# A hybrid convolution and mixture-of-experts layer: the first block of three product stages taken chunk by chunk, both token halves together

## The chip, the cores and the metric

The kernel runs on one core of one Trainium2 chip. The metric is the device time of one execution in microseconds. The kernel before has a median of 1347.25 us over three runs (1346.16 to 1347.42). All times in this text come from those runs or from one profiled execution of the kernel before.

## The reference

One layer of a decoder trunk is computed for 520 tokens of width 1024 (512 of a prompt, 8 single sample tokens), in float32:

```python
h = rmsnorm(x, g_pre1) * (1 + sc1) + sh1
z = h @ w_in                          # 1024 -> 7 * 1024: a_in a_b a_c b_val b_gate g_a g_b
v = causal_dwconv3(a_c * a_in)
y_a = (a_b * v) @ w_out_a
cv = causal_dwconv31(b_val * sigmoid(b_gate)) + b_cconv
y_b = silu(layernorm(cv)) @ w_out_b + b_out_b
m = sigmoid(g_a) * y_a + sigmoid(g_b) * y_b
t = m @ w_o
x = x + gt1 * rmsnorm(t, g_post1)
h = rmsnorm(x, g_pre2) * (1 + sc2) + sh2
x = x + gt2 * rmsnorm(moe(h), g_post2)   # 64 experts, top 8, one shared expert
```

`sc1`, `sh1`, `gt1` and their second set come from `silu(c) @ w_ada + b_ada`, per sequence.

## The kernel before

Channels lie on the 128 partitions, in C = 8 chunks of 128; the 520 tokens lie along the free axis and are taken in two halves of 260 (`half`), one PSUM bank each.

Every large matrix of the first part (`w_in`, `w_out_a`, `w_out_b`, `w_o`) is used in blocks: a block is 1024 input channels by 128 output channels. There are 80 of them, numbered n: 0 to 55 for `w_in` (four passes of a loop of 14, called f = 0 to 13), 56 to 63 for `w_out_a`, 64 to 71 for `w_out_b`, 72 to 79 for `w_o`. A block's weights come by DMA into `raw`; ScalarE copies them rounded into the high part (`split_hi`, L648), GpSimd subtracts to get the low part (`split_lo`, L460). Two such pairs fit in `wsplit`.

The activations are split in the same way, chunk by chunk, into a high and a low tensor of the product's type:

- for `w_in`: VectorE applies scale and shift (L974), ScalarE rounds (`h_hi`, L655, counted by `h_act`), VectorE subtracts (`h_lo`, L979, counted by `h_lo_dve`);
- for `w_out_a`: GpSimd multiplies `va` (L466), ScalarE rounds (`va_hi`, L669, `va_hi_act`), GpSimd subtracts (`va_lo`, L471, `va_lo_pool`);
- for `w_o`: VectorE makes the rounded sum (`m_hi`, L1089), the full sum (L1090) and the difference (`m_lo`, L1092, `m_lo_dve`).

A block is computed by `split_product` as three products per chunk and half (high x high, low x high, high x low; L1396, L1397, L1398), which makes 3 x 8 x 2 = 48 matmuls of 260 columns. It does the whole first half (24 matmuls into one bank), and then the whole second half (24 into the next bank). The blocks alternate between banks 0/1 and 2/3. For blocks f = 0 and 56 the first half waits before each chunk until that chunk's low part is there; block 72 waits for all eight low parts before its first matmul.

After block 0 TensorE computes a part of the conditioning (`ada_chunk`, L1349), which waits for four copies by ScalarE (`stB_act`, L660), and after block 56 the channel means of the convolution (`stat`, L1337), which wait for a small VectorE product (`p2_dve`, L1046).

Each engine has its own instruction stream in program order, and the streams meet only in semaphores. Nothing reorders the matmuls: the order is the order of the code.

## Time and profile before

| | |
|---|---|
| median of 3 runs | 1347.25 us |
| the profiled execution | 1346.86 us, of which the span of the profile is 1345.1 us |
| TensorE busy | 1258.6 us (94%), 9215 matmuls |
| VectorE, ScalarE, GpSimd busy | 500.5 (37%), 351.3 (26%), 368.3 us (27%) |
| the 80 blocks | from 58.1 to about 585 us |
| the expert part | from about 656 to 1273 us |

The profile shows times of one execution. Matmuls are pipelined: a record lasts about 0.28 us at the full clock, while the next one starts 0.12 us later, so spacing is read from the starts. "Granted clock" (PEclk) is the share of full speed that TensorE was given. "Idle before" is the time for which an engine had nothing to do ahead of an instruction, with what ended it.

### The profile page before, as it was taken

Reading aid. Unit: us, or ns where it says so; the run is one execution under the profiler, and the core shown is the slowest. Engines: PE = TensorE matmul, PEld = TensorE weight load, DVE = VectorE, ACT = ScalarE, POOL = GpSimd, SP = SyncE. Lnnn points to the kernel's source line nnn. Section 1 sums busy time; section 2 is a strip of 40 time slices with the busy share of each in tenths; the row PEclk is TensorE's granted clock in tenths of the full one; section 3 lists DMA queues with packets and bytes.
Section 4 is the critical chain, followed back from the end, with each engine's and each line's share of the span. In section 5 each row is a group of like instructions: output and inputs, shape, how many; then the busy total and the mean of one; then the engine's idle time right before and its main releaser. Section 6 shows DMA issues by size and latency. Waiting matters only on the chain.

```text
span 1345.1 us, 26176 instructions
## 1 busy us (share of the span) xinstructions
PE 1258.6 (94%) x9215; PEld 936.2 (70%) x9216; DVE 500.5 (37%) x857; ACT 351.3 (26%) x644; POOL 368.3 (27%) x370
## 2 busy tenths in 40 slices
PE   6799999999998998978898999998999999999985
PEld 4599999999998898967654555554555555555532
DVE  0556677566865557048412111100011100110067
ACT  4332332323232611335211122112122112211221
POOL 1144444444564333301311122112122112211200
PEclk8699999999999998989999999999999999999998
DMA  9944262443411232309599899999999999995186
GB/s 308 262 148 151 79 217 82 152 140 94 140 47 48 73 98 78 95 21 387 216 417 366 319 392 411 391 418 418 417 418 399 402 346 419 418 409 196 49 303 268
DMA packets 155591, 336.72 MB, mean 250 GB/s; under 512 B 12445, under 2 KB 96925, under 8 KB 137078
## 3 DMA queue, kind: packets, MB, share of 16 engines
q1 hardware_dynamic: 137888, 295.00, 58.6%
q0 software_dynamic: 14256, 34.10, 6.7%
q10 hardware_dynamic: 3406, 7.05, 1.6%
q8 instruction: 28, 0.46, 0.1%
q14 instruction: 13, 0.11, 0.0%
HBM read 321.65 MB, written 33.26 MB: 264 GB/s over the span
## 4 chain that ended last, share of the span: by engine, by line
PE 79%; DMA 6%; issue 5%; DVE 5%; ACT 2%; POOL 1%; SPq 1%; ACTq 0%; DVEq 0%; POOLq 0%
PE ps L1579 25%; PE ps L1591 13%; PE ps L1396 10%; PE ps L1397 10%; PE ps L1398 10%; PE ps L1572 4%; PE ps L1337 2%; PE ps L1525 2%; DMA w<-in_w_dram 2%; DMA ring<-in_w_ada_dram 2%; PE ps L1349 1%; PE ps L1585 1%; SPq L281 1%; DVE ring L1300 1%; POOL wsplit L460 1%
## 5 line engine op out<-in xcount | busy, mean ns | idle before, releaser
L1579 PE MATMUL ps<-w,xe 128*64 x3136 | 353.5, 384 | 21.9 <-issue 21.9
L1579 PEld LDWEIGHTS ps<-w,xe 128*64 128x64 f32 x3136 | 229.4, 139 | 161.3 <-issue 59.9
L1396 PE MATMUL ps<-h_s_hi,wsplit 128*128 128x260 f32 x1024 | 292.1, 285 | 2.8 <-DVE h_lo_m_hi L979 2.7
L1398 PE MATMUL ps<-h_s_hi,wsplit 128*128 128x260 f32 x1024 | 289.7, 283 | 0.0
L460 POOL TENSOR_TENSOR wsplit<-ring,wsplit 128x1024 fp32r<-128x1024 f32 x80 | 192.3, 2404 | 321.8 <-ACT wsplit L648 321.8
L1397 PE MATMUL ps<-h_lo_m_hi,wsplit 128*128 128x260 f32 x896 | 253.9, 283 | 0.0
L1266 DVE TENSOR_TENSOR rs<-sg,ps 128x128 f32<-128x128 f32 x98 | 23.8, 284 | 495.5 <-PE ps L1579 495.5
L1396 PEld LDWEIGHTS ps<-h_s_hi,wsplit 128*128 128x128 f32 x1024 | 193.6, 189 | 11.2 <-issue 6.7
L1398 PEld LDWEIGHTS ps<-h_s_hi,wsplit 128*128 128x128 f32 x1024 | 194.0, 189 | 0.0
L1591 PE MATMUL ps<-w,eactT 128*64 (+1 forms) x784 | 179.0, 598 | 0.0
L1397 PEld LDWEIGHTS ps<-h_lo_m_hi,wsplit 128*128 128x128 f32 x896 | 169.8, 190 | 0.0
L648 ACT ACTIVATE wsplit<-ring 128x1024 fp32r<-128x1024 f32 x80 | 84.8, 1060 | 322.2 <-PE ps L1398 314.9
L1014 DVE SCALAR_TENSOR_TENSOR ps<-conv,vecs,ps 128x512 f32<-128x512 f32 x224 | 154.6, 744 | 0.0
L532 POOL COPY gidx<-idxT 128x1 int32 (+1 forms) x50 | 9.2, 185 | 408.7 <-PE ps L1572 407.3
L1591 PEld LDWEIGHTS ps<-w,eactT 128*64 128x64 f32 x784 | 52.1, 136 | 89.8 <-issue 84.0
L883 ACT ACTIVATE act<-ps 128x1024 f32<-128x1024 f32 x50 | 51.2, 1024 | 162.9 <-PE ps L1591 160.4
L898 ACT ACTIVATE eactT<-ps 128x128 f32<-128x128 f32 x98 | 23.3, 278 | 188.5 <-PE ps L1585 188.5
L1572 PE MATMUL ps<-ident,scr 128*128 128x128 f32 x400 | 65.8, 287 | 0.0
L1572 PEld LDWEIGHTS ps<-ident,scr 128*128 128x128 f32 x400 | 52.3, 193 | 18.9 <-issue 17.7
L535 POOL DMA_INDIRECT scr<-h_rows,gidx x50 | 53.0, 1061 | 40.5 <-POOL gidx L532 40.5
L545 POOL DMA_INDIRECT y_rows<-act,sidx x49 | 49.9, 1019 | 40.3 <-POOL sidx L542 39.5
L895 ACT ACTIVATE sg<-ps 128x256 f32<-128x256 f32 x49 | 18.9, 385 | 148.3 <-PE ps L1579 148.3
(286 smaller groups left out, 1402.6 us busy)
## 6 DMA issues: line engine op xcount, KB each, us to landing
w<-in_w_dram SPq DMA_DIRECT2D x192, 1024.0 KB, 17.2
ring<-in_w_in_dram SPq DMA_DIRECT2D x56, 512.0 KB, 3.9
ring<-in_w_ada_dram SPq DMA_DIRECT2D x12, 2048.0 KB, 9.7
ring<-y_rows SPq DMA_DIRECT2D x8, 1024.0 KB, 9.3
act<-y_rows SPq DMA_DIRECT2D x8, 1024.0 KB, 13.9
ring<-in_w_out_a_dram SPq DMA_DIRECT2D x8, 512.0 KB, 3.6
ring<-in_w_out_b_dram SPq DMA_DIRECT2D x8, 512.0 KB, 3.7
ring<-in_w_o_dram SPq DMA_DIRECT2D x8, 512.0 KB, 3.6
```

The lines of the kernel that those rows point to most:

```text
L460: pool.tensor_tensor(wsplit[:, b, 1], raw[raw_slot], wsplit[:, b, 0], ALU.subtract).then_inc(S["w_lo"], 1)
L535: pool.indirect_dma_start(out=xg, out_offset=None, in_=h2_rows, in_offset=bass.IndirectOffsetOnAxis(ap=gidx[:, u:u + 1], axis=0), bounds_c ...
L545: pool.indirect_dma_start(out=y_rows, out_offset=bass.IndirectOffsetOnAxis(ap=sidx[:, u:u + 1], axis=0), in_=yb[:, u, :], in_offset=None, ...
L648: act.activation(wsplit[:, b, 0], raw[raw_slot], ACT.Copy).then_inc(S["w_hi"], 1)
L883: act.activation(yb[:, 1 - u, :], ps[:, 4:6, :].rearrange("p b n -> p (b n)"), ACT.Copy).then_inc(S["ex_yd"], 1)
L1014: chain(stt(out=acc[k % 2] if k != KC - 2 else cvj, in0=glu[:, k:k + NP], scalar=vecs[:, ds(j + (V_WC + 8 * k), 1)], in1=acc[k % 2], op0=A ...
L1396: mm(ps[:, bank + h, 0:HT], wsplit[:, b, 0, k, :], hi[:, k, p:q], start=(k == 0), stop=False)
L1397: mm(ps[:, bank + h, 0:HT], wsplit[:, b, 0, k, :], lo[:, k, p:q], start=False, stop=False)
L1398: ins = mm(ps[:, bank + h, 0:HT], wsplit[:, b, 1, k, :], hi[:, k, p:q], start=False, stop=(k == C - 1))
L1572: ins = tr(ps[:, h, (c % 4) * P:(c % 4 + 1) * P], v[:, c, :], ident[:, :])
L1579: ins = mm(ps[a * STRIP:(a + 1) * STRIP, bank, 0:FE], xe[:, k, a * STRIP:(a + 1) * STRIP], w[a][:, k, :], start=(k == 0), stop=(k == C - 1))
L1591: ins = mm(ps[a * STRIP:(a + 1) * STRIP, 4 + h, :], eactT[:, k, a * STRIP:(a + 1) * STRIP], w[a][:, k, h * 512:(h + 1) * 512], start=(k == ...
```

## The change

A new helper, `first_product`, replaces `split_product` for block f = 0 of each of the four passes of the loop, for block 56 and for block 72. For each chunk it issues first the four matmuls that need only the high part of the activations (two weight parts times two halves), after a wait for the chunk's high part, and then the two matmuls (two halves) that need the low part, after a wait for the low part. With `apart=3` (block 56) the low parts of the last three chunks come after all high ones. Block 72 no longer waits for all of `m_lo`, and its wait for the last merged chunk (`m_done` 17) moves to the block after it. One increment is added to a VectorE instruction (`m_hi_dve`), and one wait (`h_s_dve`) ahead of the loop. The number of matmuls, their sizes and operands are the same.

```diff
--- before.py
+++ after.py
@@ -249,7 +249,7 @@
                  "mean_pe cen_dve lrt_act ln_dve s_act x1_dve x1n_dve h2_act h2_s_dve logits_pe "
                  "lt_act score0_dve score_s_act mask_dve rank_pe idx_dve table_dve late_chain t_dve "
                  "g_done m_done m_chain t_cp stat_mm sqd idx_ab idx_mm hx_T hx_done "
-                 "x1t_T x1t_done x1t_dve h2_dve oneE_dve token_act turn_pool sh_mm sh_ev sh_act "
+                 "m_hi_dve x1t_T x1t_done x1t_dve h2_dve oneE_dve token_act turn_pool sh_mm sh_ev sh_act "
                  "exT xe_act xe_dve ex1 ex3 ex_sil ex_mul exA ea_act "
                  "ex_y ex_yd gcopy scopy passed yb_free es_dve es_pe y_there "
                  "diag_act yacc fin_sq fin_rt fin_out").split()
@@ -1086,7 +1086,7 @@
                             scalar=vecs[:, ds(j + V_OB, 1)], in1=gb[:, ds(j, 1), a:b].rearrange("p c t -> p (c t)"),
                             op0=ALU.add, op1=ALU.mult).then_inc(S["m_chain"], 1)
                     dve.wait_ge(S["m_chain"], j * 2 + 6)
-                    tt(hj, mj, gj, ALU.add)
+                    tt(hj, mj, gj, ALU.add).then_inc(S["m_hi_dve"], 1)
                     tt(mj, mj, gj, ALU.add).then_inc(S["m_done"], 1)
                     dve.wait_ge(S["m_done"], j + 10)
                     tt(m_lo[:, ds(j, 1), :].rearrange("p a t -> p (a t)"), mj, hj, ALU.subtract).then_inc(S["m_lo_dve"], 1)
@@ -1386,16 +1386,38 @@
                         ins = mm(ps[:, bank + h, 0:HT], w[:, k, :], src[:, k, a:b], start=(k == 0), stop=(k == C - 1))
                 return ins
 
-            def split_product(n, b, bank, hi, lo, as_they_come=None):
+            def split_product(n, b, bank, hi, lo):
 
                 pe.wait_ge(S["w_lo"], n + NU + 1)
                 for h, (p, q) in enumerate(half):
                     for k in range(C):
-                        if as_they_come and h == 0:
-                            pe.wait_ge(S[as_they_come], k + 1)
                         mm(ps[:, bank + h, 0:HT], wsplit[:, b, 0, k, :], hi[:, k, p:q], start=(k == 0), stop=False)
                         mm(ps[:, bank + h, 0:HT], wsplit[:, b, 0, k, :], lo[:, k, p:q], start=False, stop=False)
                         ins = mm(ps[:, bank + h, 0:HT], wsplit[:, b, 1, k, :], hi[:, k, p:q], start=False, stop=(k == C - 1))
+                ins.then_inc(items_used, 1)
+
+            def first_product(n, b, bank, hi, lo, hi_done, lo_done, apart=0):
+
+                pe.wait_ge(S["w_lo"], n + NU + 1)
+
+                def high(k):
+                    pe.wait_ge(S[hi_done], k + 1)
+                    for a in range(2):
+                        for h, (p, q) in enumerate(half):
+                            mm(ps[:, bank + h, 0:HT], wsplit[:, b, a, k, :], hi[:, k, p:q], start=(k == 0 and a == 0), stop=False)
+
+                def low(k):
+                    pe.wait_ge(S[lo_done], k + 1)
+                    for h, (p, q) in enumerate(half):
+                        ins = mm(ps[:, bank + h, 0:HT], wsplit[:, b, 0, k, :], lo[:, k, p:q], start=False, stop=(k == C - 1))
+                    return ins
+
+                for k in range(C):
+                    high(k)
+                    if k < C - apart:
+                        ins = low(k)
+                for k in range(C - apart, C):
+                    ins = low(k)
                 ins.then_inc(items_used, 1)
 
 
@@ -1413,6 +1435,7 @@
                     ins = mm(ps[:, 5, at:at + NSEQ], arow[:, n * P:(n + 1) * P], fold[:, :], start=True, stop=True)
                 ins.then_inc(S["ada_T"], 1)
 
+            pe.wait_ge(S["h_s_dve"], 1)
             with pe.Fori(0, C // 2) as it:
                 for jj in range(2):
                     j = it * 2 + jj
@@ -1434,11 +1457,17 @@
                             ada_chunk(it * 32 + 32, it * 2 + 5)
                         elif jj == 1 and i == 1:
                             ada_turn(1, it * 2 + 6)
-                        split_product(it * 14 + f, f % 2, 2 * (f % 2), h_hi, h_lo, "h_lo_dve" if f == 0 else None)
+                        if f == 0:
+                            first_product(it * 14, 0, 0, h_hi, h_lo, "h_act", "h_lo_dve")
+                        else:
+                            split_product(it * 14 + f, f % 2, 2 * (f % 2), h_hi, h_lo)
 
             for j in range(C):
                 pe.wait_ge(S["g_done"] if j < 2 else S["m_done"], 17 + j if j < 2 else j)
-                split_product(56 + j, j % 2, 2 * (j % 2), va_hi, va_lo, "va_lo_pool" if j == 0 else None)
+                if j == 0:
+                    first_product(56, 0, 0, va_hi, va_lo, "va_hi_act", "va_lo_pool", apart=3)
+                else:
+                    split_product(56 + j, j % 2, 2 * (j % 2), va_hi, va_lo)
                 if j == 0:
                     pe.wait_ge(S["p2_dve"], 1)
                     for c in range(C):
@@ -1464,14 +1493,17 @@
                     pe.wait_ge(S["m_chain"], it * 8 + (2 * jj + 2))
                     split_product(it * 4 + (64 + jj), jj % 2, 2 * (jj % 2), s_hi, cv_lo)
 
-            pe.wait_ge(S["m_lo_dve"], C)
-            pe.wait_ge(S["m_done"], 17)
+            pe.wait_ge(S["m_done"], 16)
             pe.wait_ge(S["tailrows_act"], 2)
             for j in range(C + 1):
                 if j < C:
                     if j >= 2:
                         pe.wait_ge(S["t_cp"], j)
-                    split_product(72 + j, j % 2, 2 * (j % 2), m_hi, m_lo)
+                    if j == 0:
+                        first_product(72, 0, 0, m_hi, m_lo, "m_hi_dve", "m_lo_dve")
+                    else:
+                        pe.wait_ge(S["m_done"], 17)
+                        split_product(72 + j, j % 2, 2 * (j % 2), m_hi, m_lo)
                 if j > 0:
                     pe.wait_ge(S["sqd"], 8 + j)
                     stat(6, scr[:, (j - 1) % 4, :], j - 1).then_inc(S["stat_mm"], 1)
```

What TensorE issues at the start of block 0, before: three matmuls for a chunk, all of the first half, `h_s_hi` being `h_hi` and `h_lo_m_hi` being `h_lo`.

```order
L1396 MATMUL ps<-h_s_hi,wsplit 128x260 [waits h_lo_dve,w_lo]
L1397 MATMUL ps<-h_lo_m_hi,wsplit 128x260
L1398 MATMUL ps<-h_s_hi,wsplit 128x260
L1396 MATMUL ps<-h_s_hi,wsplit 128x260 [waits h_lo_dve]
L1397 MATMUL ps<-h_lo_m_hi,wsplit 128x260
L1398 MATMUL ps<-h_s_hi,wsplit 128x260
L1396 MATMUL ps<-h_s_hi,wsplit 128x260 [waits h_lo_dve]
L1397 MATMUL ps<-h_lo_m_hi,wsplit 128x260
L1398 MATMUL ps<-h_s_hi,wsplit 128x260
```

And after the change: four matmuls on the high part, then two on the low part, both halves.

```order
L1407 MATMUL ps<-h_s_hi,wsplit 128x260 [waits h_act,w_lo]
L1407 MATMUL ps<-h_s_hi,wsplit 128x260 x3
L1412 MATMUL ps<-h_lo_m_hi,wsplit 128x260 [waits h_lo_dve]
L1412 MATMUL ps<-h_lo_m_hi,wsplit 128x260
L1407 MATMUL ps<-h_s_hi,wsplit 128x260 [waits h_act]
L1407 MATMUL ps<-h_s_hi,wsplit 128x260 x3
L1412 MATMUL ps<-h_lo_m_hi,wsplit 128x260 [waits h_lo_dve]
L1412 MATMUL ps<-h_lo_m_hi,wsplit 128x260
```

The second half's matmuls have moved from behind chunk 7 of the first half into each chunk, and the first four of a chunk no longer wait for the low part.

Block 56 on TensorE, before: its last waiting chunk (7), behind which the second half begins in the fourth row.

```order
L1396 MATMUL ps<-va_hi,wsplit 128x260 [waits va_lo_pool]
L1397 MATMUL ps<-va_lo,wsplit 128x260
L1398 MATMUL ps<-va_hi,wsplit 128x260
L1396 MATMUL ps<-va_hi,wsplit 128x260
L1397 MATMUL ps<-va_lo,wsplit 128x260
```

And after the change, from the high products of chunk 6 on, to the channel means behind the block.

```order
L1407 MATMUL ps<-va_hi,wsplit 128x260 [waits va_hi_act]
L1407 MATMUL ps<-va_hi,wsplit 128x260 x3
L1407 MATMUL ps<-va_hi,wsplit 128x260 [waits va_hi_act]
L1407 MATMUL ps<-va_hi,wsplit 128x260 x3
L1412 MATMUL ps<-va_lo,wsplit 128x260 [waits va_lo_pool]
L1412 MATMUL ps<-va_lo,wsplit 128x260
L1412 MATMUL ps<-va_lo,wsplit 128x260 [waits va_lo_pool]
L1412 MATMUL ps<-va_lo,wsplit 128x260
L1412 MATMUL ps<-va_lo,wsplit 128x260 [waits va_lo_pool]
L1412 MATMUL ps<-va_lo,wsplit 128x260
L1337 MATMUL ps<-act,avg 128x260 [waits p2_dve]
```

Behind the wait for the last low part stand two matmuls now, where before 27 stood.

The beginning of block 72 on TensorE, before; here `h_lo_m_hi` is `m_hi`, and the one wait stands for all eight chunks.

```order
L1396 MATMUL ps<-h_lo_m_hi,wsplit 128x260 [waits tailrows_act,w_lo,m_done,m_lo_dve]
L1397 MATMUL ps<-m_lo,wsplit 128x260
L1398 MATMUL ps<-h_lo_m_hi,wsplit 128x260
L1396 MATMUL ps<-h_lo_m_hi,wsplit 128x260
L1397 MATMUL ps<-m_lo,wsplit 128x260
```

And after the change.

```order
L1407 MATMUL ps<-h_lo_m_hi,wsplit 128x260 [waits w_lo,m_hi_dve,tailrows_act,m_done]
L1407 MATMUL ps<-h_lo_m_hi,wsplit 128x260 x3
L1412 MATMUL ps<-m_lo,wsplit 128x260 [waits m_lo_dve]
L1412 MATMUL ps<-m_lo,wsplit 128x260
L1407 MATMUL ps<-h_lo_m_hi,wsplit 128x260 [waits m_hi_dve]
L1407 MATMUL ps<-h_lo_m_hi,wsplit 128x260 x3
L1412 MATMUL ps<-m_lo,wsplit 128x260 [waits m_lo_dve]
L1412 MATMUL ps<-m_lo,wsplit 128x260
```

The wait for the eighth low part has moved from ahead of the 48 matmuls to ahead of the last two. The streams of VectorE, ScalarE and GpSimd hold the same instructions in the same order before and after.

## Rows read from the trace of the kernel before

**Rows 1.** Waits, TensorE: in total, times, longest (us).

```profile
PE ps L1396 <- DVE m_lo L1092: 5.6, 1, 5.6
PE ps L1396 <- POOL va_lo L471: 4.6, 2, 4.0
PE ps L1396 <- DVE h_lo_m_hi L979: 2.7, 3, 1.9
```

**Rows 2.** Timeline, block 0: start, us, engine, line, [idle before <-releaser].

```profile
52.82 3.43 PE L1379 MATMUL ps<-ident,act 120*128 120x120 f32 x16 [0.82 <-issue]
54.89 1.66 ACT L655 ACTIVATE h_s_hi<-act 128x512 fp32r<-128x512 f32 x3
55.60 2.37 DVE L979 TENSOR_TENSOR h_lo_m_hi<-act,h_s_hi 128x520 fp32r<-128x520 f32 x1 [0.86 <-ACT h_s_hi L655]
62.62 1.91 DVE L979 TENSOR_TENSOR h_lo_m_hi<-act,h_s_hi 128x520 fp32r<-128x520 f32 x3
63.73 1.48 ACT L660 ACTIVATE act<-ps 128x480 f32<-128x480 f32 x3
64.18 0.42 PE L1396 MATMUL ps<-h_s_hi,wsplit 128*128 128x260 f32 x1
65.48 0.42 PE L1396 MATMUL ps<-h_s_hi,wsplit 128*128 128x260 f32 x1
68.99 1.92 PE L1349 MATMUL ps<-ring,scT 128*32 128x512 f32 x16
```

**Rows 3.** Stretches: PE, PEld, DVE, ACT, POOL busy, PEclk, DMA, GB/s.

```profile
58.12:68.99 10.87, 9.90 (x48) 8.45 (x48) 6.41 (x12) 5.01 (x9) 0.00 (x0) 0.69 1.02 282
407.55:419.81 12.26, 7.69 (x50) 7.27 (x49) 7.31 (x12) 2.78 (x5) 6.10 (x4) 0.86 0.29 87
531.09:538.40 7.31, 7.31 (x49) 7.31 (x50) 0.45 (x3) 0.00 (x0) 0.00 (x0) 0.78 0.15 44
538.40:544.14 5.74, 5.74 (x50) 5.74 (x49) 0.00 (x0) 2.25 (x4) 2.40 (x1) 1.00 0.11 33
59.50:60.00 0.50, 0.22 (x2) 0.01 (x1) 0.50 (x1) 0.47 (x1) 0.00 (x0) 0.83 1.17 286
414.50:415.00 0.50, 0.00 (x0) 0.00 (x0) 0.50 (x1) 0.00 (x0) 0.50 (x1) 0.82 1.11 336
418.00:418.50 0.50, 0.50 (x5) 0.50 (x4) 0.00 (x0) 0.00 (x0) 0.00 (x0) 0.77 0.12 33
```

**Rows 4.** Timeline, block 56.

```profile
407.55 0.28 PE L1396 MATMUL ps<-va_hi,wsplit 128*128 128x260 f32 x1
410.25 0.64 ACT L669 ACTIVATE va_hi<-act 128x520 fp32r<-128x520 f32 x1 [0.36 <-POOL act L466]
412.48 2.54 POOL L471 TENSOR_TENSOR va_lo<-act,va_hi 128x520 fp32r<-128x520 f32 x2
413.74 1.36 DVE L1046 TENSOR_TENSOR ada<-ada,vecs 128x72 f32<-128x72 f32 x1 [0.21 <-DVE act L1041]
413.82 0.39 PE L1396 MATMUL ps<-va_hi,wsplit 128*128 128x260 f32 x1 [3.95 <-POOL va_lo L471]
419.81 7.17 PE L1337 MATMUL ps<-act,avg 128*128 128x260 f32 x32
```

**Rows 5.** Timeline, block 72.

```profile
526.71 2.34 POOL L460 TENSOR_TENSOR wsplit<-ring,wsplit 128x1024 fp32r<-128x1024 f32 x1 [3.33 <-ACT wsplit L648]
526.86 2.74 DVE L1089 TENSOR_TENSOR h_lo_m_hi<-act  x1 [0.17 <-DVE act L1085]
530.33 0.70 DVE L1092 TENSOR_TENSOR m_lo<-act,h_lo_m_hi  x1
531.09 0.59 PE L1396 MATMUL ps<-h_lo_m_hi,wsplit 128*128 128x260 f32 x1 [5.55 <-DVE m_lo L1092]
```

**Rows 6.** Chain of waits, two later pieces: start, us, what.

```profile
620.07 3.51 PE ps L1525 x16
914.84 25.85 DMA w<-in_w_dram
```


## Prediction

> **What bounds the kernel now.** I read the page first: TensorE is busy for 94% of the span, and in the chain of waits the product lines of the blocks and of the experts lead. So a gain must come from TensorE's own gaps and slow stretches. The waits of TensorE name three gaps at exactly the blocks that the change touches: 5.6 us for `m_lo`, 4.6 us in two waits for `va_lo`, 2.7 us in three for `h_lo` [rows 1]. Then the timeline around each [rows 2, 4, 5] shows what TensorE could have done in the gap, and the stretches [rows 3] what clock it was granted there. A block without a gap is the yardstick: block 73, from 538.40 to 544.14, takes 5.74 us at clock 1.00 [rows 3], or 0.120 us for each of its 48 matmuls. At half clock six matmuls lie between the starts 64.18 and 65.48 [rows 2], or 0.217 us each.
>
> **Block 0.** Before, the channel chunks come one by one from VectorE: the first low part is ready at 55.60 + 2.37 = 57.97, the last three of eight at 62.62 + 1.91 = 64.53 at the latest [rows 2], 0.94 us apart on the mean. TensorE spends this time on half its work, begins the second half at 65.48 and reaches the conditioning product at 68.99 [rows 2]. The clock was 0.69 on average over these 10.87 us [rows 3]: it fell at about 59.8, since the half microsecond from 59.50 reads 0.83 [rows 3], after the thin beginning, and (1 - 0.69) / 0.5 x 10.87 = 6.7 us of it went at half clock.
> After, the high products of chunk 0 can start when the transposes end, at 52.82 + 3.43 = 56.25; three high parts are there at 54.89 + 1.66 = 56.55 [rows 2]. Then each chunk brings six matmuls: 0.72 us at full clock, less than the 0.94 us between two chunks, or 1.30 us at half clock, more than it. Three cases:
> - Full clock: two matmuls are left at 64.53, the block ends at about 64.85, and then the conditioning product waits for ScalarE's copies, ready at 63.73 + 1.48 = 65.21 [rows 2]. It starts at 65.3 and 3.7 us are gained.
> - The clock falls at 59.8 as before, TensorE is then dense and gets it back about halfway through: 16 matmuls are done by then (two chunks and the third's high part), some 15 at half clock bring it to 63.3, the last 17 at full clock to 65.4. Gained 3.6.
> - Half clock until 66.5 as before: from chunk 2's low part at about 60.1, 32 matmuls of 0.217 us end at 67.05. Gained 1.9.
>
> I take 3.6, between the two first, since with twice as many matmuls per chunk the gaps that let the clock fall are mostly filled. At 65.3 I expect nothing else late: the conditioning product of before starts in the same 0.2 us in which block 0 ends, so its weights were there for some time, though how long the rows don't say; the split of the next weights starts when block 0 ends, as before.
>
> **Block 56.** Before: start 407.55, a wait of 3.95 us up to 413.82, a second shorter one, the mean product at 419.81 [rows 4]. Clock 0.86 on average; it fell at about 414.9 and was back at 418.2 [rows 3]. Without the waits the last low parts set everything: GpSimd's last two end at 412.48 + 2.54 = 415.02, the seventh's therefore at about 413.8, when TensorE goes on, and the eighth's at 415.02 [rows 4].
> After: chunks 0 to 4 whole and the high products of 5, 6, 7 are 30 + 12 = 42 matmuls, 5.0 us, up to 412.6; the last high part was ready at 410.25 + 0.64 = 410.89 [rows 4], in time. Two more for low 5 to 412.8, low 6 at 413.8, low 7 at 415.02, end about 415.3. The means need `p2_dve`, ready at 413.74 + 1.36 = 415.10 [rows 4], in time. Gained 419.81 - 415.3 = 4.5 if the clock holds. If it falls at 414.9 as before, the last two matmuls end at 415.5, and the 2.7 us up to 418.2 go at half speed, which costs the means 1.35 us: 4.3 - 1.35 = 2.95. The idle time shrinks from two long waits to about 1 and 1 us, which could go either way. I take 3.8.
>
> **Block 72.** Before: TensorE finishes block 71 after 531.09 - 5.55 = 525.54 and waits for the eighth low part, 530.33 + 0.70 = 531.03 [rows 5]. Then 48 matmuls take 7.31 us at clock 0.78 [rows 3], 1.6 us more than the yardstick, since the gap had taken the clock.
> After: seven chunks are ready at 525.5, 42 matmuls end at 530.6. The eighth high part is ready at 526.86 + 2.74 = 529.60 [rows 5]; its four end at 531.05, and the last two at 531.3. No gap, so no loss of clock. Block 73 follows at once: its weights are split at 526.71 + 2.34 = 529.05 [rows 5], its banks were read by then. It starts at 531.33 in place of 538.40 [rows 3]: gained 7.05. If the clock were half for the whole block, 48 x 0.217 = 10.4 us from 525.5 would end at 535.95, gained 2.45.
>
> **At nothing.** Three more first blocks in the loop change order with everything ready; a wait that is met costs nothing seen, as the chunks from 64.18 on, each with a wait in front, keep the 0.217 spacing of the second half [rows 2]. The new wait for `h_s_dve` is met by then, since VectorE signals it ahead of chunk 0, of which ScalarE has made the high part before 56.25; the increment on L1089 adds no instruction. Bounds: 0 to 0.1 us for each of these. The other streams are unchanged.
>
> **What is given on.** After each place every engine starts from what TensorE has done, the expert weights from the end of the blocks, so a lead should travel to the end whole. Sum: 3.6 + 3.8 + 7.05 = 14.45 us. Against the profiled execution of 1346.86 us this gives 1332.4, against the median of 1347.25 us 1332.8. I forecast 1332.8. Its own range, from the bounds: 1.9 + 2.95 + 7.05 = 11.9 up to 3.7 + 4.5 + 7.1 = 15.3, so 1332.0 to 1335.4, and with the 1.3 us by which runs of before differ 1331.0 to 1336.0.
>
> **Rivals.**
> - *The clock takes it back.* Waits between chunks leave TensorE at half clock in all three blocks: 1.9 + 2.95 + 2.45 = 7.3 us gained, 1339.9. For it: the thin chunks of block 0 did lose the clock [rows 3]. Against: six matmuls per chunk nearly fill the pitch there, and block 72 has no gap. The Trainium skill, page "TensorE: Matmul & The Clock Gate", section "Loop structure matters more than you think", says that a loop which waits for data ahead of every product goes cold, while a dense one stays warm; by it this order is the bad kind, and the result would be this rival's. The trace agrees for block 0 as it was; whether it holds with twice the work per wait no row shows.
> - *The lead is waited away later.* In the expert part one transfer of weights is on the chain for 25.85 us [rows 6]. If transfers, and not TensorE, set the end of that part, and did not start earlier, the result would be 1347. Against: they are issued only after the blocks, so they move too; most of that part's chain is matmuls.
> - *Slower.* Alternating banks from one matmul to the next, with the same weights loaded anew, could break the pipelining of load and product. 6 blocks x 48 = 288 matmuls are in the new order; it decides from 14.45 / 288 = 0.050 us each. The mean product alternates in this way and takes 7.17 us for 32 or 0.22 each [rows 4]; at that price, 288 x 0.10 = 28.8 us lost, 1361.6. Against: the shared expert's float32 product keeps to one bank, has the same width and takes 3.51 us for 16 [rows 6], the same 0.22; so the type costs this, not the order.
> - *It doesn't do what it says.* A later wait of the same block, say the split of its weights, could hold it. Block 0's and 72's were met; half of the gains lost would be 1340. Small.
>
> **How the numbers follow.** Forecast with its own range (1331.0 to 1336.0) 0.75; clock takes back much of it (1336 to 1341, the doesn't-do rival in it) 0.12; more gained than summed (under 1331) 0.07; waited away 0.03; slower 0.03. A measurement can tell 0.2%, 2.7 us, from no change. Faster by more: 0.75 + 0.12 + 0.07 = 0.94; within: 0.03; slower 0.03. The range takes in the forecast's and part of both neighbours: 1330.2 to 1338.0.
>
> **What would show it.** Right: TensorE's wait for `m_lo` is under 0.5 us and block 73 starts about 5.8 us after block 71's end instead of 12.9; the conditioning product starts near 65.3; from block 56's start to the means pass 7.8 us in place of 12.3; spacing in the new blocks stays at 0.12. Wrong: spacing over 0.15 at full clock (slower rival), half clock all through blocks 0 and 72 (clock rival), or longer waits for expert weights by as much as the lead.

## The result

The changed kernel takes 1333.28 us (median of 4 runs, 1332.19 to 1335.21), the kernel before 1346.88 us beside it (4 runs, 1346.16 to 1347.42). The ratio is 0.9901, with a 95% interval of 0.9884 to 0.9918: 13.6 us faster. Forecast were 1332.8 us.

The forecast took 14.45 us off 1347.25, and 13.6 off 1346.88 were measured, so a part of its closeness comes from the kernel before.

The profiled execution took 1333.35 us, its span 1331.6 us against 1345.1 before. TensorE's waits at the three blocks, which answer to [rows 1], are now:

```profile
PE ps L1407 <- ACT h_s_hi L655: 2.0, 1, 2.0
PE ps L1412 <- DVE h_lo_m_hi L979: 1.7, 1, 1.7
PE ps L1412 <- POOL va_lo L471: 1.7, 2, 0.9
```

The wait of 5.6 us for `m_lo` is gone, that for `va_lo` has shrunk from 4.6 to 1.7 us. L1407 are the products on the high part, L1412 those on the low part. Block 0 now waits twice, once for the first high part and once for the first low part. Its timeline, against [rows 2] (a line of three dots stands for lines left out):

```profile
55.25 0.71 PE L1407 MATMUL ps<-h_s_hi,wsplit 128*128 128x260 f32 x4 [1.97 <-ACT h_s_hi L655]
57.64 0.80 PE L1412 MATMUL ps<-h_lo_m_hi,wsplit 128*128 128x260 f32 x2 [1.67 <-DVE h_lo_m_hi L979]
58.23 1.07 PE L1407 MATMUL ps<-h_s_hi,wsplit 128*128 128x260 f32 x4
...
63.00 0.64 PE L1412 MATMUL ps<-h_lo_m_hi,wsplit 128*128 128x260 f32 x2
63.44 0.80 PE L1407 MATMUL ps<-h_s_hi,wsplit 128*128 128x260 f32 x4
...
65.49 0.40 PE L1412 MATMUL ps<-h_lo_m_hi,wsplit 128*128 128x260 f32 x2
65.82 1.92 PE L1349 MATMUL ps<-ring,scT 128*32 128x512 f32 x16
```

From 58.23 to 63.44 four chunks pass in 5.2 us, 1.30 us each, and TensorE has no gap: that is half clock, and slower than the chunks arrive. Block 56, against [rows 4]:

```profile
408.14 1.61 PE L1407 MATMUL ps<-va_hi,wsplit 128*128 128x260 f32 x12
409.58 0.40 PE L1412 MATMUL ps<-va_lo,wsplit 128*128 128x260 f32 x2
410.85 0.50 PE L1412 MATMUL ps<-va_lo,wsplit 128*128 128x260 f32 x2 [0.87 <-POOL va_lo L471]
412.14 0.51 PE L1412 MATMUL ps<-va_lo,wsplit 128*128 128x260 f32 x2 [0.79 <-POOL va_lo L471]
412.49 7.17 PE L1337 MATMUL ps<-act,avg 128*128 128x260 f32 x32
```

The twelve high products of the last three chunks stand together. Then come three pairs of low products, of which the last two wait for their low parts (0.87 and 0.79 us), and the means follow at once. Block 72, on VectorE and TensorE, against [rows 5]:

```profile
522.85 0.40 PE L1412 MATMUL ps<-m_lo,wsplit 128*128 128x260 f32 x2
523.09 0.64 PE L1407 MATMUL ps<-h_lo_m_hi,wsplit 128*128 128x260 f32 x4
523.79 0.51 PE L1412 MATMUL ps<-m_lo,wsplit 128*128 128x260 f32 x2
```

```profile
523.04 0.70 DVE L1092 TENSOR_TENSOR m_lo<-act,h_lo_m_hi  x1
```

The last pair starts 0.05 us after the eighth low part is finished at 523.74. The stretches, against [rows 3] (PE, PEld, DVE, ACT, POOL busy, granted clock, DMA, GB/s):

```profile
518.03:524.14 6.11, 6.04 (x51) 5.84 (x49) 5.35 (x8) 2.55 (x3) 2.38 (x1) 1.00 0.36 105
404.51:412.49 7.98, 6.32 (x51) 5.91 (x50) 6.19 (x12) 2.78 (x5) 6.21 (x4) 1.00 0.44 130
57.64:65.82 8.18, 8.18 (x44) 8.04 (x45) 6.50 (x12) 5.00 (x9) 0.00 (x0) 0.62 1.23 321
```

Blocks 72 and 56 kept the full clock (before 0.78 and 0.86), block 0 did not (0.62; before 0.69). From 57.0 to 63.7 its clock reads 0.50, from 63.8 on 1.00.

**Where the time went.** The same seven marks can be read in every trace: the end of the first `h_lo`, and the starts of the conditioning product, of block 56, of the means, of the small product behind block 73 and of the first expert step, and the end of the span. The stretches between them, in us, for all kernels of this text:

| kernel | first `h_lo` at | to conditioning (block 0) | to block 56 | to means (block 56) | to product behind block 73 (block 72) | to expert step | to end |
|---|---|---|---|---|---|---|---|
| before | 57.97 | 11.02 | 338.56 | 12.26 | 124.33 | 116.27 | 684.69 |
| changed | 57.58 | 8.24 | 338.69 | 7.98 | 117.42 | 116.79 | 684.90 |
| only 72 | 56.75 | 11.05 | 338.55 | 12.26 | 117.42 | 116.36 | 684.41 |
| only 56 | 58.21 | 10.85 | 338.54 | 7.97 | 124.71 | 116.42 | 685.00 |
| only 0 | 56.60 | 7.57 | 338.70 | 12.23 | 124.30 | 116.31 | 684.89 |
| waits 72 | 57.72 | 11.23 | 338.54 | 12.38 | 121.86 | 116.74 | 686.13 |
| low first | 57.91 | 8.63 | 338.68 | 9.97 | 116.43 | 116.45 | 684.83 |
| all new | 57.95 | 7.57 | 340.34 | 7.86 | 119.58 | 116.45 | 684.75 |
| filler | 58.11 | 7.61 | 338.79 | 8.23 | 117.26 | 116.88 | 687.52 |
| ACT order | 52.78 | 8.51 | 338.68 | 7.97 | 119.07 | 116.69 | 685.30 |
| POOL order | 57.33 | 7.57 | 338.70 | 7.69 | 116.04 | 116.81 | 686.06 |
| both | 52.55 | 8.61 | 338.70 | 7.67 | 116.02 | 116.24 | 685.51 |
| three | 51.78 | 8.51 | 338.79 | 6.05 | 115.97 | 116.55 | 684.95 |
| shift | 58.08 | 8.00 | 338.70 | 7.97 | 117.40 | 116.75 | 685.78 |

Block 0 gave 2.78 us, block 56 4.28, block 72 6.91. The start was 0.39 us earlier, which the change has no part in. Lost were 0.13 us in the loop, 0.52 between block 73 and the experts and 0.21 in the experts. The sum is 13.50, the difference of the spans.

One thing moves the stretch from the means to the product behind block 73 at a place that no edit touches: in it TensorE waits once for 2.07 us, for the split of a later block's weights. Behind this wait the changed kernel went at half clock for 3.4 us (0.50 from 453.0 to 456.3), and so did before (0.50 from 459.2 to 462.5). In low first, filler, POOL order, both and three the same wait cost no clock. Between the changed kernel and POOL order this is 1.38 us.

### The profile page after: what moved, and what is told of

The parts are those of the page before. It is cut to its first block, busy times and chain, and to the rows that moved or that the text cites. A ratio compares the mean times of both kernels' runs of the same rounds, so it can differ in the third digit from the quotient of the medians.

```text
span 1331.6 us, 26177 instructions
## 1 busy us (share of the span) xinstructions
PE 1254.4 (94%) x9215; PEld 931.5 (70%) x9216; DVE 499.7 (38%) x857; ACT 351.0 (26%) x644; POOL 367.9 (28%) x370
## 3 DMA queue, kind: packets, MB, share of 16 engines
q10 hardware_dynamic: 3406, 7.05, 1.6%
## 4 chain that ended last, share of the span: by engine, by line
PE 78%; DMA 6%; issue 6%; DVE 5%; ACT 2%; POOL 1%; SPq 1%; ACTq 0%; DVEq 0%; POOLq 0%
PE ps L1611 25%; PE ps L1623 13%; PE ps L1394 9%; PE ps L1395 9%; PE ps L1396 9%; PE ps L1604 4%; PE ps L1337 2%; DMA w<-in_w_dram 2%; DMA ring<-in_w_ada_dram 2%; PE ps L1407 1%; PE ps L1349 1%; PE ps L1617 1%; PE ps L1557 1%; SPq L281 1%; DVE ring L1300 1%
## 5 line engine op out<-in xcount | busy, mean ns | idle before, releaser
L1394 PE MATMUL ps<-h_s_hi,wsplit 128*128 128x260 f32 x960 | 272.2, 284 | 0.0
L1396 PE MATMUL ps<-h_s_hi,wsplit 128*128 128x260 f32 x960 | 270.7, 282 | 0.0
L1395 PE MATMUL ps<-h_lo_m_hi,wsplit 128*128 128x260 f32 x832 | 234.8, 282 | 0.0
L1394 PEld LDWEIGHTS ps<-h_s_hi,wsplit 128*128 128x128 f32 x960 | 180.6, 188 | 6.7 <-issue 6.7
L1396 PEld LDWEIGHTS ps<-h_s_hi,wsplit 128*128 128x128 f32 x960 | 180.8, 188 | 0.0
L1395 PEld LDWEIGHTS ps<-h_lo_m_hi,wsplit 128*128 128x128 f32 x832 | 156.6, 188 | 0.0
L1014 DVE SCALAR_TENSOR_TENSOR ps<-conv,vecs,ps 128x512 f32<-128x512 f32 x224 | 154.7, 744 | 0.0
```

The costliest lines, as they stand in the source:

```text
L1014: chain(stt(out=acc[k % 2] if k != KC - 2 else cvj, in0=glu[:, k:k + NP], scalar=vecs[:, ds(j + (V_WC + 8 * k), 1)], in1=acc[k % 2], op0=A ...
L1394: mm(ps[:, bank + h, 0:HT], wsplit[:, b, 0, k, :], hi[:, k, p:q], start=(k == 0), stop=False)
L1395: mm(ps[:, bank + h, 0:HT], wsplit[:, b, 0, k, :], lo[:, k, p:q], start=False, stop=False)
L1396: ins = mm(ps[:, bank + h, 0:HT], wsplit[:, b, 1, k, :], hi[:, k, p:q], start=False, stop=(k == C - 1))
```

## The experiments

Each is shown as an edit to the changed kernel. The kernel before was run beside each group of them: 1346.98 us beside only 72, only 56, only 0 and waits 72; 1346.74 beside low first, all new, filler and ACT order; 1347.92 beside POOL order, both and shift; 1346.90 beside three. So differences of about 1 us between groups say little.

**One place at a time.** Blocks 0 and 56 back to the old order, then 0 and 72, then 56 and 72:

```diff
-                            first_product(it * 14, 0, 0, h_hi, h_lo, "h_act", "h_lo_dve")
+                            split_product(it * 14, 0, 0, h_hi, h_lo, "h_lo_dve")
-                    first_product(56, 0, 0, va_hi, va_lo, "va_hi_act", "va_lo_pool", apart=3)
+                    split_product(56, 0, 0, va_hi, va_lo, "va_lo_pool")
```

> Only block 72 goes in the new way; blocks 0 and 56 are as before. Theory (each place gives its own gain, and it travels to the end whole): block 72's part in the two traces was 6.95 us, so the time is 1346.9 - 7.0 = 1339.9, and block 73 starts 5.8 us after block 71's end. Rival (the gains are not independent, the lead of the first places is partly waited away and the last place gives most of the 13.6): 1336 or less. Rival (part of this gain is a gift of the clock, which comes or not from run to run): a spread of over 3 us between runs.

> Only block 56 goes in the new way. Theory: its part in the traces was 4.3 us with the clock held, so 1342.6; with the clock lost at its end in some runs 1344. Rival (a later wait, on the split weights of block 60, takes the lead back): 1346.9.

> Only the first block of each loop pass goes in the new way. Theory: the traces put 2.8 us on block 0 (3.2 us of lead less 0.4 us of an earlier start), so 1344.1. Rival (3.6 us, the value of the sum; the profiled run had the clock fall early by chance): 1343.3. Rival (three more reordered blocks per run cost something): 1345 or more.

Measured: only 72 1338.58 us (1338.25 to 1338.67), ratio 0.9939 [0.9926, 0.9953]; only 56 1344.07 (1343.11 to 1348.70), 0.9988 [0.9977, 0.9998]; only 0 1343.66 (1342.42 to 1346.05), 0.9982 [0.9973, 0.9991]. The three gains by medians are 8.4 + 2.9 + 3.3 = 14.6 us, against 13.6 together; with intervals of 1.2 to 1.8 us each way this shows no interplay, and could hide one of a microsecond or two. The stretches are sharper: 6.91 us for block 72 and 4.29 for block 56 taken alone, against 6.91 and 4.28 together. The 8.4 us are more than the 7.0 expected, and the table says why: block 72's stretch is 117.42 us as in the changed kernel, 6.91 us less, but this run's first `h_lo` came 1.2 us earlier. Only 56 has the full 4.3 us in its trace, with the clock held in the means, yet loses 0.8 us again in the three stretches behind, and its median gains 2.9. Three of its eleven runs lie at 1346.9, 1348.3 and 1348.7; what those lost is in no trace. The eleven runs of only 0 spread over 3.6 us, and the one with a trace is the fastest. It shows block 0 at full clock:

```profile
56.60:64.20 7.60, 6.87 (x48) 5.63 (x49) 6.56 (x12) 5.17 (x10) 0.00 (x0) 1.00 1.30 340
```

At clock 1.00 the stretch is 7.57 us and block 0 gives 3.45 us. So the prediction's case of full clock occurs as well as one with a loss, in runs whose block 0 has the same instructions in the same order. Full clock from the start isn't even needed: all new and POOL order have the same block 0 and went at half clock up to 62.5 and 61.2 us (0.50 from 58.0 to 62.4 and from 57.4 to 61.1), and their stretch is 7.57 us too. What costs time is a clock that comes back late, as in the changed kernel at 63.8.

**Finer waits alone at block 72.** The old order, with a wait per chunk (blocks 0 and 56 as before):

```diff
-                        first_product(72, 0, 0, m_hi, m_lo, "m_hi_dve", "m_lo_dve")
+                        split_product(72, 0, 0, m_hi, m_lo, "m_lo_dve")
```

> Blocks 0 and 56 as before; block 72 keeps the old order (first half whole, then second half) and only gets a wait per chunk for the low part instead of one for all eight. This tells the finer waits from the order with both halves. Theory: 21 of 48 matmuls (2.5 us) come before the last chunk, 27 (3.2 us) behind it, where the new order leaves 2; the gap is 3 us with a thin stretch, so block 73 starts at about 534.3 on the scale of before in place of 538.4 if the clock holds and 536 if it falls: a gain of 2.5 to 4.1, time 1342.8 to 1344.4. Rival (the finer waits are all there is to it): 7 us gained, 1339.9, as with only block 72 in the new way.

Measured: 1345.38 us (1343.59 to 1346.34), ratio 0.9985 [0.9976, 0.9994]. The theory's time was missed: the median gains 1.6 us and lies 1 us above its range. In the trace, of the slowest of the eleven runs, block 72 gains 2.47 us, the lower end of what the theory gave. TensorE (first fence) and the stretch behind the wait (second):

```profile
531.14 0.58 PE L1396 MATMUL ps<-h_lo_m_hi,wsplit 128*128 128x260 f32 x1 [3.07 <-DVE m_lo L1092]
```

```profile
531.10:535.90 4.80, 4.76 (x27) 4.76 (x28) 0.50 (x3) 0.00 (x0) 0.00 (x0) 0.64 0.23 71
```

The 27 matmuls behind the last low part take 4.8 us at clock 0.64 where they would take 3.2 at full clock. The new order leaves two there, and no gap that costs the clock. The order with both halves is worth 4.4 of the 6.9 us. The last stretch of this kernel is 1.4 us longer than before's. Most of this is in the first expert step, 9.88 us in place of 8.75, at clock 0.50 from 657.5 to 664.2.

**Both halves together, high products not ahead.**

```diff
-                    pe.wait_ge(S[hi_done], k + 1)
+                    pe.wait_ge(S[lo_done], k + 1)
```

> The changed kernel, but each chunk's six matmuls wait for its low part; the high products no longer start ahead. This tells 'both halves per chunk' from 'high products ahead of the low part'. Theory (the halves are most of it): block 0 begins at the first low part with six matmuls instead of two, at half clock 0.9 us later; block 56 has ten matmuls behind the last low part instead of two, 1 us later; block 72 six instead of two, 0.4 us later. Sum 2.3 us: 1335.6. Rival (the high products ahead keep the clock up and carry the gain): 1339 or more.

Measured: 1333.77 us (1333.10 to 1334.67), ratio 0.9903 [0.9889, 0.9918]. By the stretches block 0 is 0.39 us longer and block 56 1.99 longer, and block 72 takes 6.58 us in place of 6.11. That is 2.85 us, the theory's kind of loss. Block 56:

```profile
411.53 0.91 PE L1407 MATMUL ps<-va_hi,wsplit 128*128 128x260 f32 x4 [2.05 <-POOL va_lo L471]
412.86 1.24 PE L1407 MATMUL ps<-va_hi,wsplit 128*128 128x260 f32 x4 [0.42 <-POOL va_lo L471]
413.89 1.50 PE L1412 MATMUL ps<-va_lo,wsplit 128*128 128x260 f32 x6
```

The ten matmuls behind the last low part cost 1 us, the half clock at the end the other. But the whole is only 0.5 us above the changed kernel by medians, 1.3 by the profiled runs. The stretch up to block 73 was 0.99 us shorter in spite of the longer block 72, since the clock held behind the wait of 2.07 us in it (1.00 from 453.0 to 456.3, where the changed kernel has 0.50). The theory's 1335.6 was missed by this; that the halves are most of the gain stands. What `apart=3` is worth by itself was not tried.

**Is the order itself free?** All blocks in the new order, no wait added:

```diff
-                for h, (p, q) in enumerate(half):
-                    for k in range(C):
-                        mm(... wsplit[:, b, 0, k, :], hi[:, k, p:q] ...)
-                        mm(... wsplit[:, b, 0, k, :], lo[:, k, p:q] ...)
-                        ins = mm(... wsplit[:, b, 1, k, :], hi[:, k, p:q] ...)
+                for k in range(C):
+                    for a in range(2):
+                        for h, (p, q) in enumerate(half):
+                            mm(... wsplit[:, b, a, k, :], hi[:, k, p:q] ...)
+                    for h, (p, q) in enumerate(half):
+                        ins = mm(... wsplit[:, b, 0, k, :], lo[:, k, p:q] ...)
```

> The changed kernel with the other 74 blocks in the same order too (per chunk four high and two low matmuls over both halves), without any wait added. Theory (the order itself is free; the bank may alternate and the same weights may be loaded twice in a row): 1333.3, within 1 us, and 5.74 us per block. Rival (the stretch from the conditioning product to block 56, which holds three reordered blocks with 16 waits each, is 0.14 us longer than before, 0.05 us per block; if the order is the cause and not the waits): 74 x 0.05 = 3.7 us more, 1337.

Measured: 1335.13 us (1332.50 to 1338.79), ratio 0.9913 [0.9899, 0.9927]. The stretch to block 56, which holds 52 more reordered blocks, is 1.65 us longer than in the changed kernel: 0.03 us per block, near the 0.13 us for three blocks there. Of the rest, the clock took more than the order: the first 4 us of the means went at clock 0.57 here and at 1.00 in the changed kernel. So the order costs about 0.03 us per block of 48 matmuls, under 1 ns each, and not the 0.1 us per matmul of the rival priced at 1361.6 us. The median lies between the theory (1333.3) and its rival (1337), and the six runs spread over 6.3 us.

**Does the thin beginning take the clock?** Nine unused matmuls ahead of block 0:

```diff
+            for _ in range(9):
+                mm(ps[:, 2, 0:P], avg[:, :], ident[:, :], start=True, stop=True)
             pe.wait_ge(S["h_s_dve"], 1)
```

> The changed kernel with nine matmuls (float32, 128 columns, into a bank that block 1 clears) between the transposes and block 0, where TensorE has 2 us to wait. They compute nothing that is used. Theory (block 0 lost its clock through the thin stretch before the first low part; at full clock it ends with the last low part): in runs where the filler keeps the clock, 0.6 to 1 us less than the changed kernel, 1332.5. Rival (the clock falls anyway because of the 1.7 us ahead of the first low part, or the filler delays the first high products): 1333.3 to 1334.

Measured: 1336.16 us (1335.17 to 1337.13), ratio 0.9922 [0.9909, 0.9935]. In its own place this trace is as the theory had it:

```profile
58.17:65.60 7.43, 6.86 (x44) 5.61 (x44) 6.50 (x12) 5.04 (x10) 0.00 (x0) 1.00 1.31 343
```

Clock 1.00, block 0 at 7.61 in place of 8.24 us. It is one trace. For it speaks that the changed kernel, waits 72, low first and shift, whose clock had risen at the same point (53 to 54 us), all fell back to half at about 57; against it, that only 0, all new and POOL order reached 7.57 us without a filler. Yet the kernel is 2.9 us slower, which neither theory had. The chain of waits of the changed kernel at the first expert step (start, us, what) has one piece:

```profile
646.70 8.81 PE ps L1611 x64
```

and that of the filler kernel three ("issue" is time in which TensorE waited for nothing that the profile shows):

```profile
646.88 2.04 PE ps L1613 x10
648.92 1.66 issue
650.59 8.14 PE ps L1613 x54
```

**Nine matmuls at another place**, ahead of the expert loop:

```diff
+            for _ in range(9):
+                mm(ps[:, 2, 0:P], avg[:, :], ident[:, :], start=True, stop=True)
             at_step = pe.alloc_register("step_pe")
```

> The changed kernel with the nine unused matmuls of the filler run, but placed ahead of the expert loop, where TensorE waits 3.9 us; block 0 is left alone. In the filler run block 0 kept its clock and became 0.6 us shorter, yet the whole was 2.9 us longer: the first expert step took 2.04 + 1.66 (idle, nothing waited for) + 8.14 us in place of 8.81. Theory (the loss belongs to where the expert loop's code lies in TensorE's program, which nine matmuls shift, and not to the filler at block 0): the first expert step is again long, 1336. Rival (the loss came from the filler's place): 1333.3.

Measured: 1334.49 us (1334.05 to 1336.41), ratio 0.9909 [0.9890, 0.9927].

```profile
646.89 1.50 PE ps L1611 x10
648.39 1.94 issue
650.33 6.20 PE ps L1611 x54
```

The same pause stands after the same ten matmuls, with block 0 untouched. So it comes with the nine matmuls ahead of the loop in the program and not with the filler's place. What it is stays open. The total of 1336 was missed, since the filler stands in TensorE's idle time here and the step behind it ran at clock 1.00 (0.76 in the filler kernel): the step is 9.6 us long, against 11.8 and 8.8. So of the filler kernel's 3.0 us in this step the pause is 1.66, and the rest is clock.

**What sets block 0 now?** ScalarE stood 7.6 us for the transfer of block 1's weights ahead of rounding `h`:

```diff
-            split_hi(1, 1, 16)
             for c in range(C):
                 act.wait_ge(S["h_dve"], c + 1)
                 mark(act.activation(h_hi[:, c, 0:NP], hT[:, c, 0:NP], ACT.Copy), "h_act")
+            split_hi(1, 1, 16)
```

> The changed kernel with one move on ScalarE: the split of block 1's weights, which waits for its transfer until 53.5 us, goes behind the rounding of the eight chunks of h. The first chunk of h stands ready on VectorE at about 50.8 us. Theory (the supply of h now sets block 0, and it hangs on that transfer; GpSimd's subtraction then also leaves VectorE alone): h's low parts come 3 to 4 us earlier, block 1's weights are split at about 61.5, just in time, so 3 to 4 us less than the changed kernel: 1329.5 to 1330.5. Rival (block 1's weights or ScalarE's state copies become late, or the conditioning weights are not in): 1332 or more.

Measured: 1330.00 us (1327.62 to 1330.73), ratio 0.9871 [0.9857, 0.9885], 3.3 us less than the changed kernel. The first `h_lo` is there at 52.78, 4.8 us earlier, and takes 0.70 us on VectorE where it took 2.37 beside GpSimd's split [rows 2]. TensorE:

```profile
59.71 0.40 PE L1413 MATMUL ps<-h_lo_m_hi,wsplit 128*128 128x260 f32 x2
61.29 1.92 PE L1350 MATMUL ps<-ring,scT 128*32 128x512 f32 x16 [1.18 <-ACT act L661]
```

Now the conditioning product waits 1.2 us for ScalarE's copies. 4.5 us of lead reach block 56 and the means; the stretch to block 73 then takes 1.65 back, with the clock at 0.60 from 408.0 to 412.0, in the means, where the changed kernel had 1.00.

**And block 56?** GpSimd's last low parts ahead of its split for block 57:

```diff
-                        split_lo(it * 14 + (f + 2), (i + 2) % NU, f % 2)
+                        if not (jj == 1 and i == 6):
+                            split_lo(it * 14 + (f + 2), (i + 2) % NU, f % 2)
...
                                     va_rest(c)
+                        if jj == 1 and i == 6:
+                            split_lo(it * 14 + (f + 2), (i + 2) % NU, f % 2)
```

> The changed kernel with one move on GpSimd: in the last units of the loop the two low parts of va go ahead of the split of block 57's weights. Theory (block 56 is now set by GpSimd's last low part, 412.08 us in the trace of the changed kernel, and 2.4 us of the path to it are that split): the low parts are there at about 408.5 and 409.8, TensorE has its 46 other matmuls done at 409.8, the means start at 410.1 in place of 412.5: 2.3 us less, 1331.0, and no idle time that could cost the clock behind it. Rival (block 57's weights or the product before the means are late instead, or the means wait for VectorE's last convolution steps): 1332.5 to 1333.3.

> The changed kernel with both moves, on ScalarE (block 1's weights behind the rounding of h) and on GpSimd (low parts of va ahead of block 57's weights). Theory (the places are independent): 1333.3 - 4.5 - 2.3 = 1326.5, as the run with the first move alone has the clock lost behind block 56 (1.7 us) and the second move fills that idle time. Rival (they overlap): 1328.5 or more.

Measured: 1331.63 us (1330.74 to 1333.25), ratio 0.9885 [0.9866, 0.9903], and with both moves 1328.10 (1327.10 to 1329.27), 0.9860 [0.9843, 0.9878]. Both times lie between theory and rival. The low products no longer wait, and the means do; TensorE of the kernel with the one move (first fence), and its VectorE (second):

```profile
408.67 0.88 PE L1415 MATMUL ps<-va_lo,wsplit 128*128 128x260 f32 x6
411.29 2.90 PE L1340 MATMUL ps<-act,avg 128*128 128x260 f32 x12 [1.74 <-DVE ada L1049]
```

```profile
408.92 0.69 DVE L1044 TENSOR_TENSOR act<-ps,act 128x512 f32 x1
409.81 1.42 DVE L1049 TENSOR_TENSOR ada<-ada,vecs 128x72 f32<-128x72 f32 x1 [0.21 <-DVE act L1044]
```

The small product of `p2_dve` takes 1.42 us beside GpSimd's split. In the changed kernel it took 0.23: there it started at 410.71, by chance 0.04 us before GpSimd's next operation. Block 56 gained 0.3 of the expected 2.3 us, and the rival was right on the cause. The rest of the trace's gain can't be put down to the move: 1.38 us in the stretch behind, where the clock held as in low first and filler without it, and 0.67 in block 0, less 1.2 lost behind the start of the first expert step.

**The wait that was left.** Both moves, and:

```diff
-                    pe.wait_ge(S["p2_dve"], 1)
+                    pe.wait_ge(S["pa_chain"], 8 * 42)
```

> Both moves, and the channel means wait for VectorE's last convolution step (pa_chain) in place of the small product behind it (p2_dve). With the second move alone the means waited 1.74 us for that product, which took 1.42 us in place of 0.23 beside GpSimd's split; the last convolution step ended 1.68 us before the means. Theory (that product is the only thing that held them): 1.6 us less than both moves alone, 1326.5, and the means start within 0.3 us of VectorE's last convolution step. Rival (the means, now beside the blocked product, delay what VectorE has to do next, or the clock is lost elsewhere): 1328.

Measured: 1326.98 us (1324.32, 1324.52, 1329.43, 1329.66), ratio 0.9858 [0.9837, 0.9879]. TensorE and VectorE:

```profile
404.14 0.88 PE L1416 MATMUL ps<-va_lo,wsplit 128*128 128x260 f32 x6
405.13 7.06 PE L1341 MATMUL ps<-act,avg 128*128 128x260 f32 x31
```

```profile
404.38 0.69 DVE L1045 TENSOR_TENSOR act<-ps,act 128x512 f32 x1
```

The means start 0.06 us after VectorE's last convolution step, and block 56's stretch is 6.05 us, 1.62 less than with both moves, as expected, and half of what it was before. This version has the lowest median, 6.3 us under the changed kernel. Its runs fall into two pairs 5 us apart, and only one of the fast pair has a trace, so against both moves alone (1327.10 to 1329.27) the last step isn't told apart by time, only by its stretch.

## Why the prediction was right

**Block 0**, predicted 3.6 us (between 1.9 and 3.7): 2.78 in the changed kernel's trace, 3.45 in that of only 0. The first has the form of the middle case: the clock fell, TensorE was then dense at 1.30 us per chunk, and got the clock back within the block. The sizes were off. I had the first high products at 56.25, set by the transposes; here they started at 55.25 and were set by ScalarE (1.97 us of wait), as the transposes were done earlier. The clock fell at about 57.0, not at 59.8, and came back at 63.8. Counted from the first low part this is 6.2 us, where the sum had 63.3 - 57.97 = 5.3, and the 0.9 us are the 0.8 missing in the gain. That the clock comes back "about halfway through" had no row behind it: it stayed at half for 6.8 us, as long as before ([rows 3] give 6.7). From 59.8 on, 6.8 us would have been the third case, 1.9 us gained. So the middle case came near because the clock fell early, partly in a wait where it cost nothing, and that was luck.

**Block 56**, predicted 3.8, between 2.95 and 4.5: 4.28, and the clock held through block and means (1.00). The upper case was right, less 0.2 us: the last low part came 7.57 us after the block's start in place of 7.47, and the pair behind it was followed by the means 0.4 us later in place of 0.3. In low first, all new, filler and ACT order some clock was lost around here (0.57 in the first 4 us of all new's means), so the lower case exists as well. The value between the two described neither.

**Block 72**, predicted 7.05: 6.91. The clock stayed at 1.00, TensorE waited under 0.3 us (before 5.55), block 73 started 5.95 us after block 71's end (expected 5.8, before 12.9), and the finer waits alone brought 2.47.

**At nothing**: the three other first blocks cost 0.13 us together (the bound was 0 to 0.1 each). **Given on**: the lead of 14.2 us behind block 73 reached the end up to 0.7 us. 0.5 of it went in a float32 product ahead of the experts, where the clock was 0.73 in place of 0.77 over 11 us.

**The sum.** 14.45 us were forecast and 13.50 are in the traces: block 0 gave 0.82 less, block 56 0.48 more, block 72 0.14 less, the start 0.39 more, and 0.86 were lost elsewhere. That errors of both signs partly cancelled is luck too.

**The rivals.** That the clock takes it back failed at blocks 56 and 72 and held in part at block 0. The page "TensorE: Matmul & The Clock Gate" of the Trainium skill, section "Loop structure matters more than you think", calls a loop with a long DMA wait ahead of every product, 8 us in its example, the cold kind. The prediction read it more widely than it stands. No run here has such a loop: the old order of block 72 had one wait of 5.55 us ahead of 48 products, with clock 0.78 in them, and the new order has waits of 2.0 us at most, with clock 1.00 in blocks 56 and 72 and 0.62 in block 0. That the lead is waited away fell: the weights' transfer on the chain took 25.30 us after and 25.85 before [rows 6], and moved along. That alternating banks costs 0.1 us per matmul fell with all new. The last one fell too: no later wait held a block, since all three gave their gain.

## What to carry to other kernels

When a consumer takes its input in chunks as they come, put every product of a chunk behind that chunk's wait, all halves of the output included, so that the least work is left behind the last chunk; it left two matmuls there instead of 27 or 48, and in blocks 56 and 72 the clock stayed full. Finer waits without that reordering gave a third of it in the trace of block 72. Then look at what sets the supply: two instructions in program order on ScalarE and GpSimd, each needed only by a later block, were worth another 5 us. Read more than one trace before a gain of a microsecond is put down to an edit: half-clock stretches behind waits that the edit didn't touch were worth 1.4 us here.

## What the runs showed of the hardware that was not expected

- Nine matmuls more in TensorE's program, at either of two places ahead of the expert loop, came with a pause of 1.66 and 1.94 us inside the loop's first pass, after ten matmuls and with nothing waited for. The changed kernel has none there.
- A VectorE operation with both inputs in SBUF that starts while a GpSimd operation runs ends only after it: `h_lo` takes 2.37 us in place of 0.69, the product for `p2_dve` 1.42 in place of 0.23. The Trainium skill, page "SBUF — State Buffer", section "SBUF: two separate sides", tells of a pair of ports that the two engines share as an exclusive lock; by it the loser waits out the whole instruction, and the traces agree: in the changed kernel GpSimd's split ends at 54.67 + 2.36 = 57.03, and VectorE's operation, issued at 55.21, at 57.58, 0.55 us behind it, about as if it had begun only then (alone it takes 0.70):

```profile
54.67 2.36 POOL L460 TENSOR_TENSOR wsplit<-ring,wsplit 128x1024 fp32r<-128x1024 f32 x1 [6.26 <-ACT wsplit L648]
55.21 2.37 DVE L979 TENSOR_TENSOR h_lo_m_hi<-act,h_s_hi 128x520 fp32r<-128x520 f32 x1 [3.44 <-ACT h_s_hi L655]
```

The convolution steps at L1014, one of whose inputs is in PSUM, took 0.74 us beside such a split and without one. The same thing stood in block 72's old wait: the last high part (L1089) took 2.74 us beside a split [rows 5], where the same addition one line further down, into `mj`, takes 0.69. So about 2 of the 5.55 us of that wait were this, and moving GpSimd's split there was not tried; in the new order TensorE waits under 0.3 us and it costs nothing.

- The first low part came between 56.60 and 58.21 us in kernels whose VectorE, ScalarE and GpSimd have the same instructions up to there. That moves a single run by more than 1 us.
- Behind the wait of 2.07 us between the means and block 73 TensorE went at half clock for 3.4 us in some kernels (0.50 from 453.0 to 456.3 in the changed one) and kept 1.00 in others (low first), though neither the wait nor the work around it differed.
